# Second feed-forward of a diffusion step: two ordinary hidden pairs in place of three, and its token sums in a new order

## The chip, the cores and the metric

One Trainium2 chip, and one core of it. The metric is the device time of one execution in microseconds (us). The kernel before takes 1400.44 us, the median of 3 runs (1399.87 to 1401.21).

The engines of the core, as the profile names them: PE (TensorE, matmuls), PEld (its weight loads), DVE (VectorE), ACT (ScalarE), POOL (GpSimd) and SP (SyncE, which here issues the loads of weights). Each runs its own list of instructions in the order in which the program writes it, and waits on semaphores for the others.

## What is computed

One trunk layer on 128 context tokens and 512 latent tokens, 1024 channels: a feed-forward, a mixer, and a second feed-forward.

```python
def swiglu(h, w_in, w_out):
    g, u = jnp.split(h @ w_in, 2, axis=-1)
    return (jax.nn.silu(g) * u) @ w_out

def trunk_layer(...):
    h = rms_norm(x, norm_pre[0]) * (1.0 + sc1) + sh1
    x = x + 0.5 * g1 * rms_norm(swiglu(h, ffn_w_in[0], ffn_w_out[0]), norm_post[0])
    h = rms_norm(x, norm_pre[1]) * (1.0 + sc2) + sh2
    m, s_f, s_b = mixer(h, ...)
    x = x + g2 * rms_norm(m, norm_post[1])
    h = rms_norm(x, norm_pre[2]) * (1.0 + sc3) + sh3
    x = x + 0.5 * g3 * rms_norm(swiglu(h, ffn_w_in[1], ffn_w_out[1]), norm_post[2])
```

The hidden width of a feed-forward is 2816, that is 22 blocks of 128 (`FT`); `ffn_w_in` has a gate half and a value half.

## The kernel before, in words

**Numbers in two parts.** Each operand of a matmul is kept as a high part (`_hi`, type fp32r, made by a copy on ACT) and a low part (`_lo`, the full number less the high part, a subtraction on POOL or DVE). A product is three matmuls: high by high, high by low, low by high.

**Tokens** lie in columns, 640 of them (`T`), channels on the partitions in 8 blocks (`KT`). The normalized input of the second feed-forward is in `Hhi` and `Hlo`; it is made in five parts of 128 tokens (semaphores `h_32`, `h_hi`, `h_lo`), of which the last, part 4, is still being made when the feed-forward begins.

**Pairs.** One hidden block needs one slab of gate weights and one of value weights; the two are a pair. The first `EARLY_PAIRS` = 3 pairs are ordinary: in the second feed-forward they run in stage `in1A` over the first 384 tokens (`G_COLS[0]`; pair 0, then the transposes of token part 4, then pairs 1 and 2) and then in stage `in1B` over the other 256 with the weights that were kept. The remaining `SEVEN` = 19 pairs (stage `in1s`, `seven_products`) use seven products of half size in place of eight (Strassen's scheme in Winograd's form): 4 channel blocks by 320 tokens each, 12 matmuls a product, in the order

1. gate rows 0 to 3 by the tokens' quadrant b11,
2. weight sum `s2` by token sum `T2`,
3. `s1` by `T1`,
4. value rows 0 to 3 (by then a weight difference) by `T3`, added to the result of 2,
5. gate rows 4 to 7 by b21, added to 1 (gives `slab_done`),
6. value rows 4 to 7 by `T4` (gives `slab_done`),
7. `s4` by b22, added to 3.

Between them DVE forms the sums U2, U3, C22, C21, C12 out of PSUM and the two halves of the hidden block (`hid_a`, `hid_b`); product 4 waits for U2 and product 7 for C22.

**Token sums** (`token_combinations`, once for each feed-forward `f`): four whole quadrants (`whole`: high plus low) and the sums T1, T2, T3, T4, eight operations of 4 x 320 columns on DVE. ACT makes the high parts of T2, T1 and T4 (`token_highs`) and of T3 (in `seven_gates`), POOL the low parts of T2 and T1 (`token_lows`) and of T4 (in `seven_low`, behind the low half of pair 0's first gate part), DVE that of T3 (in `seven_sums`). The buffer of a token sum's full numbers is that of its low part.

**Weight sums** of a pair: `first_sums` (s1, s2 and the value difference) and `last_sum` (s4) on DVE, `gate_highs` and `value_highs` (seven copies) on ACT, `seven_low` (five subtractions) on POOL, `lows` (s2 and gate rows 4 to 7) on DVE. In the steady state this is done for pair p + 1 while pair p's products run. For pair 0 of the second feed-forward it has to be ready when stage `in1B` ends.

**DVE's order** at the start of the second feed-forward: hidden block (0, 0), then `h_affine(1, 4)` and `h_low(1, 4)` (which complete the input), hidden block (0, 1), the token sums, (0, 2), (1, 0), `first_sums`, `last_sum`, (1, 1), `lows`, (1, 2), and `seven_sums`. (0, 1) is pair 1 of `in1A`, (1, 1) that of `in1B`.

**The end of the pairs.** The hidden blocks lie in `M32`; `whole_high` (ACT) and `whole_low` (DVE) split them for the output product (`out_group`), whose slab m needs blocks 2m and 2m + 1. The ordinary blocks are split while the last pair runs, three more blocks right behind it, and then two for each slab of the output product. Weights go through a few buffers in turn (`STAGES` names them by number); a load waits until the buffer's last user is done (`FREE`), and ACT makes a slab's high part in `after_slab`.

The order on POOL matters below, so these lines of `seven_low` are quoted (564 to 569):

```python
            pool.wait_ge(sem("s_made"), 4 * p + 3)
            pool.wait_ge(sem("seven_hi"), 7 * p + 1)
            low(*(x[:, 0:KH, :] for x in gate)).then_inc(sem("seven_lo"), 1)
            if p == f * SEVEN:
                pool.wait_ge(sem("t_hi"), 3 * f + 3)
                low(*(y[:, :, :] for y in T4)).then_inc(sem("t_lo"), 1)
```

## Time and profile before

| | |
|---|---|
| median of 3 runs | 1400.44 us (1399.87 to 1401.21) |
| span of the profiled execution, first to last instruction | 1397.4 us |
| PE busy | 1376.4 us (98%), 9537 matmuls |
| DVE busy | 747.2 us (53%) |
| POOL busy | 724.6 us (52%) |
| ACT busy | 582.5 us (42%) |
| PE's share of the chain that ended last | 92% |
| second feed-forward, first matmul of each stage | `in1A` 963.88 us, `in1B` 989.76 us, `in1s` 1007.02 us |

The profile's page gives busy times, the chain that ended last and the costliest groups of instructions. The timeline gives single instructions of an engine in order of time, equal neighbours merged; the view of stretches gives each engine's busy time and the granted TensorE clock between two times. All times are us from the start of the span. A matmul's own duration covers its way through the array, so neighbours overlap: what a matmul costs PE is the time from its start to the next one's, and that is read from a stretch divided by the matmuls in it.

### The profile page before, as it was taken

Reading aid. Unit: us, or ns where it says so; the run is one execution under the profiler, and the core shown is the slowest. Engines: PE = TensorE matmul, PEld = TensorE weight load, DVE = VectorE, ACT = ScalarE, POOL = GpSimd, SP = SyncE. Lnnn points to the kernel's source line nnn. Section 1 sums busy time; section 2 is a strip of 40 time slices with the busy share of each in tenths; the row PEclk is TensorE's granted clock in tenths of the full one; section 3 lists DMA queues with packets and bytes.
Section 4 is the critical chain, followed back from the end, with each engine's and each line's share of the span. In section 5 each row is a group of like instructions: output and inputs, shape, how many; then the busy total and the mean of one; then the engine's idle time right before and its main releaser. Section 6 shows DMA issues by size and latency. Waiting matters only on the chain.

```text
span 1397.4 us, 23473 instructions
## 1 busy us (share of the span) xinstructions
PE 1376.4 (98%) x9537; PEld 1257.1 (90%) x9537; DVE 747.2 (53%) x1109; ACT 582.5 (42%) x946; POOL 724.6 (52%) x530
## 2 busy tenths in 40 slices
PE   6999999999999999999999999999999999999998
PEld 5799898999888888999999999988999999998886
DVE  5686565766702431478776312235977666675033
ACT  5243333434534663244445222257344443455243
POOL 0475545465966672324223433542576555667653
PEclk9999999999999999999999999999999999999999
DMA  9756666233545541212112222333122223334465
GB/s 344 263 171 212 218 230 211 61 92 91 177 123 173 189 173 49 61 54 62 54 42 64 76 76 76 103 109 91 46 76 83 77 83 91 91 106 153 135 195 181
DMA packets 215294, 173.34 MB, mean 124 GB/s; under 512 B 6472, under 2 KB 175636, under 8 KB 215060
## 3 DMA queue, kind: packets, MB, share of 16 engines
q1 hardware_dynamic: 212448, 170.61, 39.1%
q8 instruction: 76, 1.25, 0.4%
q10 hardware_dynamic: 2740, 1.24, 0.3%
q14 instruction: 30, 0.25, 0.1%
HBM read 168.65 MB, written 3.17 MB: 123 GB/s over the span
## 4 chain that ended last, share of the span: by engine, by line
PE 92%; DVE 2%; DMA 2%; POOL 2%; ACT 1%; SPq 1%; issue 0%; DVEq 0%; ACTq 0%; POOLq 0%
PE PP L818 33%; PE PP L616 24%; PE PP L635 9%; PE PP L637 9%; PE PP L636 9%; PE PP L674 2%; DMA W_in<-in_ffn_w_in 1%; PE PP L889 1%; PE PP L660 1%; PE PP L1015 1%; PE PP L1031 1%; POOL W_lo L543 0%; DMA W_in<-in_ffn_w_out 0%; PE PP L1085 0%; POOL O_lo L543 0%
## 5 line engine op out<-in xcount | busy, mean ns | idle before, releaser
L543 POOL TENSOR_TENSOR W_lo<-W_in,W_hi 128x512 fp32r<-128x512 f32 (+1 forms) x304 | 380.2, 1277 | 445.2 <-ACT W_hi L1223 437.9
L552 POOL TENSOR_TENSOR W_lo<-W_in,W_hi 128x512 fp32r<-128x512 f32 x112 | 176.2, 1587 | 184.2 <-ACT S_hi L1450 182.3
L1223 ACT ACTIVATE W_hi<-W_in 128x1024 fp32r<-128x1024 f32 x143 | 150.9, 1057 | 224.5 <-PE PP L637 119.9
L635 PE MATMUL PP<-W_hi,Mlo 128*128 128x512 f32 x440 | 172.1, 391 | 0.4 <-DVE W_lo L1850 0.3
L637 PE MATMUL PP<-W_hi,Mhi 128*128 128x512 f32 x440 | 171.3, 389 | 0.0
L636 PE MATMUL PP<-W_lo,Mlo 128*128 128x512 f32 x440 | 171.2, 389 | 0.0
L616 PE MATMUL PP<-Hhi,W_hi 128*128 128x320 f32 (+2 forms) x608 | 146.7, 316 | 0.0
L616 PE MATMUL PP<-Hlo,W_hi 128*128 128x320 f32 (+2 forms) x608 | 142.4, 309 | 0.0
L616 PE MATMUL PP<-Hhi,W_lo 128*128 128x320 f32 (+2 forms) x608 | 142.2, 309 | 0.0
L818 PE MATMUL PP<-Hhi,W_hi 128*128 128x320 f32 x452 | 141.2, 312 | 0.5 <-DVE TT L2007 0.5
L818 PE MATMUL PP<-Hhi,W_lo 128*128 128x320 f32 x452 | 139.7, 309 | 0.0
L818 PE MATMUL PP<-Hlo,W_hi 128*128 128x320 f32 x452 | 139.6, 309 | 0.0
L552 POOL TENSOR_TENSOR S_lo<-S_in,S_hi 128x512 fp32r<-128x512 f32 x76 | 116.1, 1528 | 0.0
L616 PEld LDWEIGHTS PP<-Hhi,W_hi 128*128 128x128 f32 x608 | 101.2, 188 | 3.9 <-issue 2.7
L616 PEld LDWEIGHTS PP<-Hlo,W_hi 128*128 128x128 f32 x608 | 102.8, 188 | 0.0
L616 PEld LDWEIGHTS PP<-Hhi,W_lo 128*128 128x128 f32 x608 | 102.7, 188 | 0.0
L635 PEld LDWEIGHTS PP<-W_hi,Mlo 128*128 128x128 f32 x440 | 82.6, 188 | 19.4 <-POOL W_lo L543 1.0
L637 PEld LDWEIGHTS PP<-W_hi,Mhi 128*128 128x128 f32 x440 | 82.6, 188 | 17.4
L636 PEld LDWEIGHTS PP<-W_lo,Mlo 128*128 128x128 f32 x440 | 82.6, 188 | 16.8
L818 PEld LDWEIGHTS PP<-Hhi,W_hi 128*128 128x128 f32 x452 | 84.8, 188 | 10.8 <-issue 9.9
L818 PE MATMUL PP<-T_hi,S_hi 128*128 128x320 f32 x304 | 93.9, 309 | 0.0
L818 PE MATMUL PP<-T_lo,S_hi 128*128 128x320 f32 x304 | 93.9, 309 | 0.0
(297 smaller groups left out, 3002.1 us busy)
## 6 DMA issues: line engine op xcount, KB each, us to landing
W_in<-in_ffn_w_out SPq DMA_DIRECT2D x176, 256.0 KB, 3.2
W_in<-in_ffn_w_in SPq DMA_DIRECT2D x84, 512.0 KB, 4.3
modl<-in_w_mod SPq DMA_DIRECT2D x14, 2048.0 KB, 8.1
W_in<-in_w_in SPq DMA_DIRECT2D x32, 512.0 KB, 3.8
modw<-in_w_mod SPq DMA_DIRECT2D x4, 2048.0 KB, 14.4
HL<-g_rows SPq DMA_DIRECT2D x6, 512.0 KB, 6.5
V_in<-in_w_in SPq DMA_DIRECT2D x10, 256.0 KB, 3.7
O_in<-in_w_out SPq DMA_DIRECT2D x10, 256.0 KB, 5.6
```

The source lines that it names most:

```text
L543: return nc.gpsimd.tensor_tensor(lo[:, k0:k1, :], full[:, k0:k1, :], hi[:, k0:k1, :].bitcast(fp32), ALU.subtract)
L552: return nc.gpsimd.tensor_tensor(lo, full, hi.bitcast(fp32), ALU.subtract)
L616: m = mm(out[:, 0:c1 - c0], w[:, k, :], src[:, c0:c1], start=lead and n == 0 and a == 0, stop=tail and n == len(x) - 1 and a == 2)
L635: mm(out, xh, wh, start=lead and kk == 0, stop=False)
L636: mm(out, xh, wl, start=False, stop=False)
L637: m = mm(out, xl, wh, start=False, stop=tail and kk == 1)
L660: return nc.tensor.transpose(out, in_, ident[0:k, 0:k])
L674: m = mm(PP[3][32 * q:32 * q + 32, 0, :], S2[:, k, 30 - 2 * i:62 - 2 * i], w[:, k, :], start=first and k < 4, stop=k >= 4, skip_group_chec ...
L818: m = mm(out, wk[:, k, :], xk[:, k, :], start=not add and k == 0 and a == 0, stop=k == KH - 1 and a == 2, skip_group_check=add)
L889: m = mm(PP[n][:, half, 0:HALF], w[:, k, :], src[:, half * HALF:(half + 1) * HALF], start=k == 0 and a == 0, stop=k == KT - 1 and a == 2)
L1015: m = mm(near(pair_of(hd, lev))[32 * q:32 * q + 32, ch, :], KX[lev % 2][:, at:at + 32], queries, start=True, stop=True)
L1223: A(W[i][0], W[i][2], ACT.Copy).then_inc(hi_done, 1)
```

## The change

- `EARLY = (3, 2)`: the second feed-forward has 2 ordinary pairs and 20 pairs with seven products, the first keeps 3 and 19. The counts of semaphores follow from `SEVEN_AT`, `SEVEN_END` and `HIDDEN`.
- Buffers: `in1A` and `in1B` use four; pair 0 of `in1s` uses 12 and 9 as before, pair 1 uses 0 and 8, then 1, 2, 12, 0 in turn.
- DVE, token sums of the second feed-forward: the two quadrants of the first 320 tokens are made ahead of hidden block (0, 0), in the place of T1's and T4's full numbers. After (0, 1) come one quadrant, T1, the other quadrant, T2 and T4. T3 comes later, behind `last_sum`, and hidden block (1, 1) behind `lows`.
- ACT: T1's high part and `gate_highs` after the gate of (0, 1); T2's high part, `value_highs` and then T4's high part after the gate of (1, 0).
- POOL: T1's low part first, then T2's; each waits also until the sums that read the full numbers are made. T4's stays where it was, and T3's stays on DVE.
- At the end of the pairs two blocks are split during the last pair (three before), and the three behind it are 2, 3 and 4 (before: 3, 4 and 5).

```diff
-EARLY_PAIRS = 3
+EARLY = (3, 2)
-SEVEN = FT - EARLY_PAIRS
+SEVEN = tuple(FT - e for e in EARLY)
+SEVEN_AT = (0, SEVEN[0])
+SEVEN_END = (SEVEN[0], SEVEN[0] + SEVEN[1])
+HIDDEN = (EARLY[0], EARLY[0] + EARLY[1], EARLY[0] + 2 * EARLY[1])
...
-    ("in1A", 2 * EARLY_PAIRS, KEEP[:2] + [1, 2, 0] + KEEP[2:3], False),
-    ("in1B", 2 * EARLY_PAIRS, KEEP[:2] + [1, 2, 0] + KEEP[2:3], True),
-    ("in1s", 2 * SEVEN, [12, 9] + [1, 2, 0, 12] * SEVEN, False),
+    ("in1A", 2 * EARLY[1], KEEP[:2] + [1, 2], False),
+    ("in1B", 2 * EARLY[1], KEEP[:2] + [1, 2], True),
+    ("in1s", 2 * SEVEN[1], [12, 9, 0, 8] + [1, 2, 12, 0] * SEVEN[1], False),
...
-            for n, x in enumerate((T2, T1)):
+            for n, x in enumerate(first_tokens(f)):
+                pool.wait_ge(sem("t_made"), 4 * f + (2, 3)[n])
                 pool.wait_ge(sem("t_hi"), 3 * f + n + 1)
                 low(*(y[:, :, :] for y in x)).then_inc(sem("t_lo"), 1)
...
+                if (grp, j) == (0, 1):
+                    token_high(1, T1)
+                    gate_highs(1, 0)
                 if (grp, j) == (1, 0):
-                    token_highs(1)
-                if (grp, j) == (1, 1):
-                    gate_highs(1, 0)
+                    token_high(1, T2)
                     value_highs(1, 0)
+                    token_high(1, T4)
...
+        def second_tokens_first_half():
+            dve.wait_ge(slab_done, BASE["in1A"])
+            dve.wait_ge(sem("h_lo"), NCH + 3)
+            dve.wait_ge(sem("h_hi"), NCH + 3)
+            whole(0, 0, T1[2])
+            link(whole(KH, 0, T4[2]))
+
+        def second_tokens_t1_t2_t4():
+            t3, bsum = T3_IN[1], BSUM[1]
+            dve.wait_ge(sem("h_lo"), 2 * NCH)
+            dve.wait_ge(sem("h_hi"), 2 * NCH)
+            link(whole(0, HALF, t3))
+            V.tensor_tensor(T1[2][:, :, :], t3[:, :, :], T1[2][:, :, :], ALU.subtract).then_inc(sem("t_made"), 1)
+            whole(KH, HALF, bsum).then_inc(sem("b22_whole"), 1)
+            dve.wait_ge(sem("t_made"), 5)
+            dve.wait_ge(sem("b22_whole"), 1)
+            V.tensor_tensor(T2[2][:, :, :], bsum[:, :, :], T1[2][:, :, :], ALU.subtract).then_inc(sem("t_made"), 1)
+            dve.wait_ge(sem("t_made"), 6)
+            V.tensor_tensor(T4[2][:, :, :], T2[2][:, :, :], T4[2][:, :, :], ALU.subtract).then_inc(sem("t_made"), 1)
+
+        def second_tokens_t3():
+            t3, bsum = T3_IN[1], BSUM[1]
+            V.tensor_tensor(t3[:, :, :], bsum[:, :, :], t3[:, :, :], ALU.subtract).then_inc(sem("t_made"), 1)
...
+        second_tokens_first_half()
         early_hidden(0, 0)
         h_affine(1, 4)
         h_low(1, 4)
         early_hidden(0, 1)
-        token_combinations(1)
-        early_hidden(0, 2)
+        second_tokens_t1_t2_t4()
         early_hidden(1, 0)
         first_sums(1, 0)
         last_sum(1, 0)
+        second_tokens_t3()
+        lows(1, 0)
         early_hidden(1, 1)
-        lows(1, 0)
-        early_hidden(1, 2)
         seven_sums(1)
```

## Rows read from the trace of the kernel before

**Rows 1.** The page: busy times, and the chain that ended last, by engine.
```profile
PE 1376.4 (98%) x9537; PEld 1257.1 (90%) x9537; DVE 747.2 (53%) x1109; ACT 582.5 (42%) x946; POOL 724.6 (52%) x530
...
PE 92%; DVE 2%; DMA 2%; POOL 2%; ACT 1%; SPq 1%; issue 0%; DVEq 0%; ACTq 0%; POOLq 0%
```

**Rows 2.** Stretches: start:end, length, PE busy (x matmuls), granted clock, DMA share, GB/s.
```profile
973.02:989.76 16.74, 16.74 (x100) 1.00 0.00 1
989.76:1007.02 17.26, 17.26 (x145) 1.00 0.29 85
1007.02:1020.29 13.27, 12.83 (x86) 1.00 0.17 50
1020.29:1032.61 12.32, 12.32 (x86) 1.00 0.16 45
```

**Rows 3.** Timeline of PE at product 4 of pair 0: start, length, instruction, idle before.
```profile
1012.88 0.41 PE L818 MATMUL PP<-Hhi,I_hi 128*128 128x320 f32 x1 [0.41 <-POOL I_lo L552]
```

**Rows 4.** Timeline of DVE, start of the second feed-forward.
```profile
970.67 0.16 DVE L1829 RECIPROCAL ST<-ST 128x1 f32<-128x1 f32 x1 [1.45 <-ACT ST L1303]
...
978.79 1.22 DVE L1842 TENSOR_TENSOR Hlo<-HL,Hhi 128x1024 fp32r<-128x1024 f32 x1 [1.13 <-ACT Hhi L1313]
981.64 0.56 DVE L2316 TENSOR_TENSOR M<-TT,PP 128x384 f32<-128x384 f32 x1 [1.62 <-PE PP L616]
982.11 1.65 DVE L1908 TENSOR_TENSOR BSUM<-Hhi,Hlo 128x1280 f32<-128x1280 f32 x1
...
985.20 1.49 DVE L1919 TENSOR_TENSOR T_in<-T_in,BSUM 128x1280 f32<-128x1280 f32 x1
...
996.04 0.69 DVE L1937 TENSOR_TENSOR S_in<-I_in 128x512 f32<-128x512 f32 x1
996.76 3.35 DVE L1941 TENSOR_TENSOR S_in<-S_in,W_in 128x512 f32<-128x512 f32 x1
1000.03 3.45 DVE L1942 TENSOR_TENSOR I_in<-W_in,I_in 128x512 f32<-128x512 f32 x1
...
1004.00 0.41 DVE L2316 TENSOR_TENSOR M<-TT,PP 128x256 f32<-128x256 f32 x1
...
1005.71 3.46 DVE L1965 TENSOR_TENSOR W_lo<-W_in,W_hi 128x512 fp32r<-128x512 f32 x1
...
1009.42 2.25 DVE L1996 TENSOR_TENSOR Hlo<-T_in,Hhi 128x1280 fp32r<-128x1280 f32 x1
1011.60 0.47 DVE L2007 TENSOR_TENSOR TT<-TT,PP 128x320 f32<-128x320 f32 x1
```

**Rows 5.** Timeline of POOL, the low parts for pair 0 of `in1s`.
```profile
996.38 6.55 POOL L552 TENSOR_TENSOR T_lo<-T_in,T_hi 128x1280 fp32r<-128x1280 f32 x2 [13.96 <-ACT T_hi L1462]
1003.56 1.69 POOL L552 TENSOR_TENSOR W_lo<-W_in,W_hi 128x512 fp32r<-128x512 f32 x1 [0.63 <-DVE I_in L1942]
1005.19 3.43 POOL L552 TENSOR_TENSOR T_lo<-T_in,T_hi 128x1280 fp32r<-128x1280 f32 x1
1008.59 1.74 POOL L552 TENSOR_TENSOR S_lo<-S_in,S_hi 128x512 fp32r<-128x512 f32 x1
1010.29 4.24 POOL L552 TENSOR_TENSOR I_lo<-I_in,I_hi 128x512 fp32r<-128x512 f32 x2
```

**Rows 6.** Timeline of ACT, high parts: of the token sums, of pair 0.
```profile
995.04 3.58 ACT L1462 ACTIVATE T_hi<-T_in 128x1280 fp32r<-128x1280 f32 x3
...
998.87 1.14 ACT L1442 ACTIVATE W_hi<-W_in 128x512 fp32r<-128x512 f32 x2
```

**Rows 7.** Timelines of PE and DVE: first feed-forward's output product, slabs 0 to 2.
```profile
343.93 0.39 PE L635 MATMUL PP<-W_hi,Mlo 128*128 128x512 f32 x1
...
351.13 3.54 DVE L1983 TENSOR_TENSOR Mhi<-M,Mlo 128x640 fp32r<-128x640 f32 x2 [3.00 <-ACT Mlo L1355]
...
352.29 0.47 PE L635 MATMUL PP<-W_hi,Mlo 128*128 128x512 f32 x1
```

**Rows 8.** Stretches of PE alone behind its last matmul, columns as in rows 2.
```profile
1391.90:1396.30 4.40, 0.01 (x1) 1.00 0.56 218
1396.30:1397.40 1.10, 0.00 (x0) 0.51 0.21 80
```

More of the change, by code:

```diff
@@ L123, in plan @@
         free[base["woA"] + n] = after
-    for n, after in ((0, base["woA"]), (1, base["woA"] + 1)) + ((5, base["in1A"] - 1),):
+    for n, after in ((0, base["woA"]), (1, base["woA"] + 1)):
         free[base["in1A"] + n] = after
@@ L128, in plan @@
     free[base["in1s"] + 1] = base["in1A"] - 1
+    free[base["in1s"] + 3] = base["in1A"] - 1
     return base, buf, free, order, need, fresh
@@ L368, in early_bank, with first_tokens @@
         return ((4, 0), (6, 2))[grp][j % 2] + u
+    def first_tokens(f):
+        return (T1, T2) if f else (T2, T1)
     def ring_entries():
@@ L373, in ring_entries @@
         entries = []
-        for _ in range(SEVEN):
+        for _ in range(max(SEVEN)):
             entries.append((RING[s1], RING[s2], RING[s4]))
@@ L485, in _ @@
         load(BASE["in0s"], 0, KT, w0[:, :, j * P:(j + 1) * P])
-        for p in range(1, SEVEN):
-            j = EARLY_PAIRS + p
+        for p in range(1, SEVEN[0]):
+            j = EARLY[0] + p
             load_pair(BASE["in0s"] + 2 * p, w0, j)
@@ L520, in _ @@
         w1 = ffn_w_in[0, 1].rearrange("(k p) n -> p k n", p=P)
-        for j in range(EARLY_PAIRS):
+        for j in range(EARLY[1]):
             load_pair(BASE["in1A"] + 2 * j, w1, j)
-        for j in range(EARLY_PAIRS, FT):
-            load_pair(BASE["in1s"] + 2 * (j - EARLY_PAIRS), w1, j)
+        for j in range(EARLY[1], FT):
+            load_pair(BASE["in1s"] + 2 * (j - EARLY[1]), w1, j)
         wo1 = ffn_w_out[0, 1].rearrange("(k p) n -> p k n", p=P)
@@ L584, in _ @@
             if i in (BASE["out0A"], BASE["out1A"]):
-                for p in range(SEVEN):
+                for p in range(SEVEN[int(i == BASE["out1A"])]):
                     seven_low(int(i == BASE["out1A"]), p)
@@ L843, in seven_products @@
                 pe.wait_ge(sem("hid_a"), p - 1)
+            if first and f:
+                pe.wait_ge(sem("gate_ready"), HIDDEN[1])
             product(x, quadrant(gate, 0, KH), b11).then_inc(sem("product"), 1)
@@ L918, in _ @@
         late_mods(2)
-        for j in range(1, EARLY_PAIRS):
+        for j in range(1, EARLY[0]):
             if j == 1:
@@ L934, in _ @@
         last_mod = MOD_LATE - len(MOD_AFTER) - 1
-        for p in range(SEVEN):
+        for p in range(SEVEN[0]):
             seven_products(0, p)
@@ L1181, in _ @@
         pe.wait_ge(sem("h_lo"), NCH + 3)
-        for j in range(EARLY_PAIRS):
+        for j in range(EARLY[1]):
             if j == 0:
@@ L1197, in _ @@
         pe.wait_ge(sem("h_lo"), 2 * NCH)
-        for j in range(EARLY_PAIRS):
+        for j in range(EARLY[1]):
             for u in range(2):
@@ L1202, in _ @@
                 if j > 1:
-                    pe.wait_ge(sem("hid_ready" if u else "gate_ready"), 2 * EARLY_PAIRS + j - 1)
+                    pe.wait_ge(sem("hid_ready" if u else "gate_ready"), HIDDEN[1] + j - 1)
                 slab(i, (bank(early_bank(1, j, u)),), h_tiles, (G_COLS[1],)).then_inc(slab_done, 1)
-        for p in range(SEVEN):
+        for p in range(SEVEN[1]):
             seven_products(1, p)
@@ L1334, in out_group @@
                 if b != 1 and grp == 0:
-                    for j in range(EARLY_PAIRS + 2 * m + 3, min(FT, EARLY_PAIRS + 2 * m + 5)):
+                    e = EARLY[b // 2]
+                    for j in range(e + 2 * m + 3, min(FT, e + 2 * m + 5)):
                         whole_high(b // 2, j)
@@ L1470, in seven_gates @@
             act.wait_ge(slab_done, BASE[SEVENTHS[f]])
+            act.wait_ge(sem("t_made"), 4 * f + 4)
             A(T3[0], T3_IN[f][:, :, :], ACT.Copy).then_inc(sem("t3_hi"), 1)
-            for p in range(SEVEN):
+            for p in range(SEVEN[f]):
                 i, _, _ = seven_slabs(f, p)
                 x = seven_banks(f, p)[0]
-                n = f * SEVEN + p
+                n = SEVEN_AT[f] + p
                 if p:
@@ L1486, in seven_gates @@
                 else:
-                    for j in range(EARLY_PAIRS):
+                    for j in range(EARLY[f]):
                         whole_high(f, j)
@@ L1504, in _ @@
             if j == 1:
-                token_highs(0)
+                for x in (T2, T1, T4):
+                    token_high(0, x)
             if j == 2:
@@ L1693, in _ @@
             c0, c1 = G_COLS[grp]
-            for j in range(EARLY_PAIRS):
-                n = (1 + grp) * EARLY_PAIRS + j
+            for j in range(EARLY[1]):
+                n = HIDDEN[grp] + j
                 after_slab(BASE[stage] + 2 * j)
@@ L1910, in token_combinations @@
         def token_combinations(f):
[L1911 to L1915 removed]
+            dve.wait_ge(sem("h0_ready"), KT)
             t3, bsum = T3_IN[f], BSUM[f]
@@ L1996, in seven_sums @@
             V.tensor_tensor(T3[1], T3_IN[f][:, :, :], T3[0].bitcast(fp32), ALU.subtract).then_inc(sem("t3_lo"), 1)
-            for p in range(SEVEN):
+            for p in range(SEVEN[f]):
                 i, _, _ = seven_slabs(f, p)
                 x, y, z, v = seven_banks(f, p)
-                n = f * SEVEN + p
+                n = SEVEN_AT[f] + p
                 if p:
@@ L2022, in seven_sums @@
                 V.tensor_tensor(A_C22, A_U3, z, ALU.add).then_inc(sem("c22_done"), 1)
-                if p + 1 < SEVEN:
+                if p + 1 < SEVEN[f]:
                     lows(f, p + 1)
                 else:
-                    whole_low(f, 1)
-                    whole_low(f, 2)
+                    for j in range(1, EARLY[f]):
+                        whole_low(f, j)
                 dve.wait_ge(slab_done, i + 2)
```

94 lines of the change are left out of this document (43 added, 51 removed).

## The prediction

> **What bounds the kernel now.** I read the page first. PE is busy for 98% of the span and holds 92% of the chain that ended last [rows 1], so the time is the number of PE's matmuls by their pitch, plus the few stalls of PE. An edit can win only by taking matmuls off PE, and lose only by making PE wait. Next I read PE's pitch in both kinds of pair from the view of stretches, which shows the 384-column, 256-column and 320-column stages apart [rows 2]. Last I read the timelines of DVE, POOL and ACT from 970 to 1012 us, where pair 0 of the seven-product stage is prepared, and asked how much earlier than PE each piece is ready. That slack is small: product 4 of pair 0 already starts late behind POOL's low half of the value slab [rows 3]. It starts at 1012.88 where 36 matmuls behind 1007.02, at 0.147 us each, would put it at 1012.30; there is no slack left at this point.
>
> **What the change takes off PE.** An ordinary pair is 48 matmuls of 384 columns and 48 of 256. 973.02 to 989.76 holds two pairs of the first kind, 8.37 us each; 989.76 to 1007.02 holds three of the second, 5.75 us each [rows 2]. Together 14.12 us. A seven-product pair is 84 matmuls in 12.32 us, the last stretch of that view [rows 2]. One pair changes its kind, so PE saves 14.12 - 12.32 = 1.80 us, with everything else hidden. That is all there is to win, 0.13%. But stage in1s now begins 14.12 us earlier, at 1007.02 - 14.12 = 992.90, and the preparation of pair 0 has to be done 14.12 us earlier too.
>
> **When the preparation can begin.** The input is complete with the last low part at 978.79 + 1.22 = 980.0 [rows 4]. The early half of the token sums, two operations of about 1.5 us, fits behind 970.83, where DVE is idle until hidden block (0, 0); I cost it at nothing, and if that idle time were gone it would cost nothing still, since DVE next waits for PE at 981.64 [rows 4]. This wait does not move: it is for pair 1 of in1A. From the start of the next operation at 982.11 [rows 4] I walk the new order, at a pitch of 1.5 us per token operation:
> - DVE: quadrant to 983.7, T1 to 985.2, quadrant to 986.7, T2 to 988.2, T4 to 989.7, hidden block (1, 0) to 990.1 (0.41 us [rows 4]).
> - ACT: T1's high part (3.58 us for three, so 1.2 us [rows 6]) to 986.5, then gate_highs, T2's high part to 989.5.
> - POOL may write T1's low part only when T2 is made, 988.2. Before, the first token low part started at 996.38 [rows 5]. The two-part order thus gains 8.1 us here, not 14.12.
>
> **How DVE and POOL share.** A low part of 1280 columns takes POOL 3.28 us (6.55 for two [rows 5]). DVE's weight sums of 512 columns take 0.69 us when POOL is idle and 3.35 and 3.45 us when POOL makes token low parts [rows 4]: each ends about half a microsecond behind the end of a POOL operation (996.38 + 3.28 = 999.66, against 1000.11; 1002.93 against 1003.48). So I count one such DVE operation per POOL operation. Hidden blocks and PSUM sums stay at 0.41 to 0.5 us beside a busy POOL (1004.00 in [rows 4] lies inside 1003.56 to 1005.25 in [rows 5]). The Trainium skill, SBUF — State Buffer, section "Who interferes with whom", says that a DVE instruction with two SBUF inputs and a GpSimd one that reads SBUF exclude each other, the second to issue waiting for the first. By it, too, moving DVE's sums beside POOL's token low parts buys little.
>
> **Pair 0, step by step.**
> 1. T4 and T1's low part become ready together at 988.2; whichever goes first, T1's low part and T2's are done at about 996.2 (988.2 + 1.5 + 3.2 + 3.4).
> 2. DVE: s1 gets through at 993.4, s2 at 996.8, the value difference, with POOL idle, at 997.5.
> 3. POOL: gate rows 0 to 3 wait for that difference: 997.6 + 1.69 [rows 5] = 999.25. **PE's product 1 starts at 999.3 where it could at 992.90: a stall of 6.4 us.** Before, this low part was ready at 1005.25, 1.8 us ahead of PE.
> 4. ACT: value_highs is five copies from 996.9 at a pitch of 0.52 us (two take 1.14, one 0.62 [rows 6]), and T4's high part stands behind them, to 1000.8. POOL, in order, waits for it, then takes 3.43 us [rows 5]: T4's low part done at 1004.3. Before: 1008.62.
> 5. From here the pattern of before repeats, 4.2 to 4.3 us earlier: s1's low part (1.74), value rows (2.1 each) [rows 5]; DVE's gate rows 4 to 7 (3.46), T3's low part (2.25), U2 (0.47) [rows 4]. T3 and s2's low part fit between 998 and 1001.3, so product 2 runs behind product 1.
> 6. Product 3 waits for s1's low part, 1006.1. Product 4 starts at 1012.88 - 4.2 = **1008.7**; without any stall it would be 992.90 + 5.28 = 998.2. PE has lost 10.5 us there.
>
> Behind product 4 both kernels do the same with the same neighbours: 12.32 us for the added pair, and what was at 1012.88 is at 1008.7. Shift so far: -4.2 + 12.32 = +8.1 us.
>
> **The end of the pairs.** With two ordinary blocks, block 5 leaves the group of three behind the last pair and becomes the first of slab 0's two, and output slab 2 waits for it. The buffers of the new order also free the third output slab half a pair later. The first feed-forward has that buffer order now: its first block of that place is split from 351.13, two in 3.54 us, and slab 2 starts at 352.29 [rows 7], 0.17 us late by the pitch of 0.227 us (36 matmuls behind 343.93, the stage's first [rows 7]), held by the weights. There it was block 6, which slab 2 doesn't need; block 5 would be ready at 351.13 + 1.7 = 352.85. I take 0.7 us; bounds 0 (the split uncontended, 0.8 us) and 1.5 us (it waits for one POOL operation more). SP's loads move with the slabs' users; pair 1's two are free when the mixer's output ends, before 970 us, so no load is on the path. I cost that at nothing; a late load would be 2 us at most (within the upper end).
>
> **The sum.** 8.1 + 0.7 = +8.8 us. The profiled execution has a span of 1397.4 us and the median of the runs is 1400.44, 3.0 us more; I add the shift to both: span 1406.2, **1409.2 us** for the median.
>
> **Bounds of the preparation.** The long DVE operations are the unknown. Below: none of them waits (rival 2), +2.5 us. Above: POOL loses another 1.5 us to DVE in T1's and T2's low parts and one DVE operation (3.4 us) lands ahead of U2: +12.
>
> **The rivals.**
> 1. *Hidden after all* (the other side: not slower). If pair 0's gate low part is ready by 992.90 and the others keep PE's pace, the change gives -1.80 + 0.7 = -1.1: 1399.3 us. It decides at that one time. For it speaks only that DVE and POOL are about half idle over the span [rows 1]. Against it: T2 is made at 988.2, and the two token low parts (6.5 us) and a gate part (1.3 us) stand in POOL's queue before it, 996.0 even without contention. Chance 4%.
> 2. *POOL's queue without the exclusion*: T1 and T2 low to 994.7, gate to 996.0, T4 to 999.2, s1 to 1000.5, value rows 0 to 3 to 1001.8, products 3 and 4 from 1000.6 and 1002.4. Then 1002.4 - 1012.88 + 12.32 + 0.7 = +2.5: 1402.9 us. The durations of 3.35 to 3.46 us speak against it. Chance 8%.
> 3. *The clock falls in the stall.* Behind PE's last matmul, near 1391.9, the granted clock is 1.00 up to 1396.30 and 0.51 behind [rows 8], so behind 4.4 us of idleness PE fell to 1.2 GHz there, and the stall is 6.4. At half the clock products 1 and 2 would take 3.5 us each: product 3 would start at 1006.3 against 1006.1, and if it is slow too, product 4 at 1009.8. Cost 0 to 1.5 us, so 1410.5 us. Most of it hides in the wait that is there anyway. The Trainium skill, TensorE: Matmul & The Clock Gate, section "HAM oscillation — how this bites in real kernels", describes this chain of wait and slow restart; it speaks against the change. Chance 20%.
> 4. *The preparation takes longer than the copied pattern*: 1411 to 1413 us, chance 8%.
>
> **How the numbers follow.** My forecast has 60%. Its own range is 1406.5 to 1411.5. The range is 1403.5 to 1412.5, which leaves out rivals 1 and 2 and part of 4. Within 0.2% (2.8 us, about what a measurement of this kernel can tell from no change) is 1397.6 to 1403.2: rivals 1 and 2, 11%. Faster by more isn't reached even with all hidden; I keep 1% of rival 1's 4 for it, for an output stage that gains as well. Slower: 88%.
>
> **What the new profile would show.** PE idle from about 992.9 to 999.3 ahead of the first 320-column matmul of in1s, released by POOL's low part of the gate slab; a second gap ahead of product 3 (some 3 us) and a small one ahead of product 4; T1's low part starting near 988.3; DVE's s1 and s2 near 3.3 us long; a gap of POOL near 999 to 1001 ended by T4's high part; pair 1's first matmul near 1016; a short gap at output slab 2. I am wrong if s1 and s2 take 0.7 us beside the token low parts, or if product 1 starts before 997.

## The result, and the profile after

The changed kernel takes 1408.24 us, the median of 4 runs (1407.34 to 1409.29), against 1400.64 us for the kernel before beside it (4 runs, 1399.87 to 1401.21). The ratio is 1.0059, with a 95% interval of 1.0047 to 1.0071: 7.6 us slower, 0.54%, where 8.8 us were forecast. The profiled execution has a span of 1406.5 us at a mean granted clock of 0.996. It is slower, and by nearly the forecast amount; but two of the terms were off in opposite directions, and one rival, the fall of the clock, came true in its first part.

The page of the changed kernel first, its busy times and its chain, to be read against [rows 1]:

```profile
PE 1377.5 (98%) x9525; PEld 1257.7 (89%) x9525; DVE 753.4 (54%) x1120; ACT 584.6 (42%) x952; POOL 729.3 (52%) x531
...
PE 90%; DVE 3%; DMA 2%; ACT 2%; POOL 1%; SPq 1%; issue 1%; DVEq 0%; ACTq 0%; POOLq 0%
```

PE has 12 matmuls fewer (one pair's 96 have become 84) and its share of the chain falls from 92% to 90%. Its busy time has not fallen, although it does less, since part of it ran at half the clock. The groups of PE's waits say where it stood still. Columns: engine and tile, line, who ended the wait, total us, times, longest.

```profile
PE PP L827 <- POOL W_lo L560: 5.6, 1, 5.6
PE PP L644 <- DVE Mhi L2021: 2.4, 3, 1.6
...
PE PP L827 <- POOL I_lo L560: 0.5, 1, 0.5
```

The first line is product 1 of pair 0 waiting for the low half of the gate slab. The second is mostly in the output product, which had no wait for DVE in its first slabs before. The third is product 4. PE's timeline places them (start, length, instruction, idle before):

```profile
991.97 0.28 PE L625 MATMUL PP<-Hhi,W_lo 128*128 128x256 f32 x1
997.84 0.63 PE L827 MATMUL PP<-Hhi,W_hi 128*128 128x320 f32 x1 [5.58 <-POOL W_lo L560]
...
1003.94 0.31 PE L827 MATMUL PP<-T_hi,S_lo 128*128 128x320 f32 x1
1004.26 0.41 PE L827 MATMUL PP<-T_hi,S_hi 128*128 128x320 f32 x1
...
1006.76 0.41 PE L827 MATMUL PP<-Hhi,I_hi 128*128 128x320 f32 x1 [0.48 <-POOL I_lo L560]
...
1256.22 0.39 PE L646 MATMUL PP<-W_hi,Mhi 128*128 128x512 f32 x1
1257.22 0.50 PE L644 MATMUL PP<-W_hi,Mlo 128*128 128x512 f32 x1 [0.61 <-DVE Mhi L2021]
...
1277.53 0.39 PE L646 MATMUL PP<-W_hi,Mhi 128*128 128x512 f32 x1
1279.53 0.50 PE L644 MATMUL PP<-W_hi,Mlo 128*128 128x512 f32 x1 [1.62 <-DVE Mhi L2021]
```

The last matmul of `in1B` starts at 991.97; at its pitch of 0.12 us product 1 could start at 992.09 and starts at 997.84: 5.7 us lost. Product 3 follows product 2 at 1004.26, product 4 starts at 1006.76 where it started at 1012.88 before [rows 3]. Output slab 2 loses 0.77 us (1257.22 - 1256.22 - the pitch of 0.227), slab 7 loses 1.77 (1279.53 - 1277.53 - 0.227).

What made product 1 late is in the timelines of DVE and POOL, which answer to [rows 4] and [rows 5]:

```profile
985.77 1.49 DVE L1957 TENSOR_TENSOR T_in<-BSUM,T_in 128x1280 f32<-128x1280 f32 x1
987.30 1.49 DVE L1959 TENSOR_TENSOR T_in<-T_in 128x1280 f32<-128x1280 f32 x1
988.71 0.41 DVE L2352 TENSOR_TENSOR M<-TT,PP 128x256 f32<-128x256 f32 x1
989.04 3.12 DVE L1975 TENSOR_TENSOR S_in<-I_in 128x512 f32<-128x512 f32 x1
992.20 3.25 DVE L1979 TENSOR_TENSOR S_in<-S_in,W_in 128x512 f32<-128x512 f32 x1
995.37 0.68 DVE L1980 TENSOR_TENSOR I_in<-W_in,I_in 128x512 f32<-128x512 f32 x1
```

```profile
987.34 7.56 POOL L560 TENSOR_TENSOR T_lo<-T_in,T_hi 128x1280 fp32r<-128x1280 f32 x2 [12.10 <-DVE T_in L1957]
996.13 1.65 POOL L560 TENSOR_TENSOR W_lo<-W_in,W_hi 128x512 fp32r<-128x512 f32 x1 [1.23 <-DVE I_in L1980]
999.44 3.07 POOL L560 TENSOR_TENSOR T_lo<-T_in,T_hi 128x1280 fp32r<-128x1280 f32 x1 [1.66 <-ACT T_hi L1473]
```

POOL starts T1's low part when DVE has made T2 (985.77 + 1.49 = 987.26), does both token parts in 7.56 us, and is free at 994.90. DVE's s1 and s2 take 3.12 and 3.25 us beside it, the value difference 0.68 behind it. The gate's low part waits for that difference, runs from 996.13 to 997.78, and product 1 starts 0.06 us later.

**Which time to hold the sum against.** In the profile of after the first matmul of `in1A` comes at 963.04, before at 963.88. Nothing ahead of it was edited, and over the thirteen profiled executions of this study it lies between 962.97 and 964.83. So below I give times from that matmul (t = 0), read from each kernel's timeline of PE:

| kernel | product 1 | product 4 | output product | end of span | output to end |
|---|---|---|---|---|---|
| before | 43.14 | 49.00 | 278.17 | 433.53 | 155.36 |
| after | 34.80 | 43.72 | 285.22 | 443.47 | 158.25 |

Product 4 comes 5.28 us sooner and one seven-product pair of 12.32 us [rows 2] is added behind it: +7.04, and the output product starts at +7.05. From there to the end the changed kernel loses 2.89 us more. Together +9.94 us in the part that was edited. The metric shows 7.6. Of the difference, 0.84 us is the upstream scatter between the two profiled executions, which leaves +9.1 between their spans (1406.5 - 1397.4). Some 0.4 us lies outside the span: 1.76 to 1.84 us in all four executions of after, 2.19 to 2.30 us in 43 executions of the kernel before that ran beside the experiments. The rest would be that the profiled execution of before was a short one: with 2.2 us outside, the median execution of before has a span near 1398.4, 1.0 us above the profiled one's 1397.4. But the spans of those four executions are not on record, and the 1.0 is worked out from their median, so 9.94 - 0.84 - 1.0 - 0.4 = 7.7 closes by construction and shows nothing.

The later runs speak for the larger number. The two kernels of the section on the clock take the same time from t = 0 to the end as the changed kernel within 0.2 us (443.27 and 443.63 against 443.47), and they are 9.0 and 9.7 us slower than the kernel before on their own chips. The interval of the changed kernel reaches from 6.6 to 9.9 us and holds both. So the loss is 7.6 us as measured here, and probably nearer the 9.5 (9.94 - 0.4) of the traces.

### The profile page after: what moved, and what is told of

Same layout as the page of the kernel before. It is cut to its first block, busy times and chain, and to the rows that moved or that the text cites. A ratio compares the mean times of both kernels' runs of the same rounds, so it can differ in the third digit from the quotient of the medians.

```text
span 1406.5 us, 23487 instructions
## 1 busy us (share of the span) xinstructions
PE 1377.5 (98%) x9525; PEld 1257.7 (89%) x9525; DVE 753.4 (54%) x1120; ACT 584.6 (42%) x952; POOL 729.3 (52%) x531
## 4 chain that ended last, share of the span: by engine, by line
PE 90%; DVE 3%; DMA 2%; ACT 2%; POOL 1%; SPq 1%; issue 1%; DVEq 0%; ACTq 0%; POOLq 0%
PE PP L827 34%; PE PP L625 23%; PE PP L644 8%; PE PP L646 8%; PE PP L645 8%; PE PP L683 2%; PE PP L900 1%; DMA W_in<-in_ffn_w_in 1%; PE PP L669 1%; PE PP L1026 1%; DMA W_in<-in_ffn_w_out 1%; PE PP L1042 1%; POOL W_lo L551 0%; DVE Mhi L2021 0%; PE PP L1096 0%
## 5 line engine op out<-in xcount | busy, mean ns | idle before, releaser
L827 PE MATMUL PP<-Hhi,W_hi 128*128 128x320 f32 x460 | 144.4, 314 | 6.0 <-POOL W_lo L560 5.6
L827 PE MATMUL PP<-Hhi,W_lo 128*128 128x320 f32 x460 | 142.8, 310 | 0.0
L827 PE MATMUL PP<-Hlo,W_hi 128*128 128x320 f32 x460 | 142.7, 310 | 0.0
L625 PE MATMUL PP<-Hhi,W_hi 128*128 128x320 f32 (+2 forms) x592 | 141.7, 316 | 0.0
L625 PE MATMUL PP<-Hlo,W_hi 128*128 128x320 f32 (+2 forms) x592 | 137.4, 309 | 0.0
L625 PE MATMUL PP<-Hhi,W_lo 128*128 128x320 f32 (+2 forms) x592 | 137.3, 309 | 0.0
L560 POOL TENSOR_TENSOR S_lo<-S_in,S_hi 128x512 fp32r<-128x512 f32 x78 | 119.3, 1530 | 0.0
L625 PEld LDWEIGHTS PP<-Hlo,W_hi 128*128 128x128 f32 x592 | 99.6, 188 | 0.0
L827 PE MATMUL PP<-T_hi,S_hi 128*128 128x320 f32 x312 | 97.0, 311 | 0.0
L827 PE MATMUL PP<-T_hi,S_lo 128*128 128x320 f32 x312 | 96.9, 311 | 0.0
```

Of the source, the lines that this page charges most:

```text
L560: return nc.gpsimd.tensor_tensor(lo, full, hi.bitcast(fp32), ALU.subtract)
L625: m = mm(out[:, 0:c1 - c0], w[:, k, :], src[:, c0:c1], start=lead and n == 0 and a == 0, stop=tail and n == len(x) - 1 and a == 2)
L827: m = mm(out, wk[:, k, :], xk[:, k, :], start=not add and k == 0 and a == 0, stop=k == KH - 1 and a == 2, skip_group_check=add)
```

## The experiments

The question was not whether it is slower but which of the edits costs, and whether the mechanism named in the prediction is the one: DVE and POOL excluding each other in front of pair 0 (my theory), or POOL's queue alone, or the clock. All diffs are against the changed kernel. The three groups of runs were on different chips; ratios are to runs of the kernel before on the same chip (medians 1400.15, 1398.88 and 1399.93 us). Times in us of different groups can't be set side by side, only what each kernel is over its own before.

Most effects below are 2 to 3 us, and four executions of a kernel scatter by up to 4 us, so they are read from t = 0 in one profiled execution of each kernel. The medians do not show them: the changed kernel is 7.6 us over before, and the four kernels whose traces are 2.0 to 3.1 us shorter from t = 0 are 7.5 (one more split), 8.3 (without T4's low part), 6.8 (sums first) and 8.4 us (low parts on DVE) over theirs.

### The two halves of the change

The new order with the old number of pairs (the buffers of the stages and the loads' order go back too):

```diff
-EARLY = (3, 2)
+EARLY = (3, 3)
...
         second_tokens_t1_t2_t4()
+        early_hidden(0, 2)
         early_hidden(1, 0)
...
         early_hidden(1, 1)
+        early_hidden(1, 2)
```

> Three ordinary pairs as before, with the new order of token sums and high and low parts. Theory (POOL's queue of low parts bounds pair 0, and the new order starts it earlier): token low parts start near 988 in place of 996.4, all of pair 0's low parts are ready before PE's product 1, the stall of 0.57 us ahead of product 4 and that of 0.2 us ahead of product 7 go, nothing else moves: 0.5 to 0.8 us faster than before, about 1399.9 us. Rival (the order itself costs, for instance by the early sums delaying the last token part): 1401 us or more.

Measured: 1398.29 us (10 runs), ratio 0.9987, interval 0.9978 to 0.9997. The order alone is not slower; it is a trifle faster. In its trace product 4 comes at t = 48.41 against 49.00 before, the output product at 277.21, 0.96 us sooner. The two small waits of pair 0 are gone, since T1's low part starts at t = 24.5, eight us sooner than the first token low part before (996.38 [rows 5], t = 32.5), while PE arrives no sooner (t = 43.13):

```profile
987.49 4.27 POOL L559 TENSOR_TENSOR T_lo<-T_in,T_hi 128x1280 fp32r<-128x1280 f32 x1 [5.95 <-DVE T_in L1956]
...
998.49 1.68 POOL L559 TENSOR_TENSOR W_lo<-W_in,W_hi 128x512 fp32r<-128x512 f32 x1 [1.95 <-DVE I_in L1979]
```

The gate's low part is ready at 1000.17, some 6 us ahead of PE.

The two pairs with the old order of the sums (the orders of high parts on ACT and of low parts on POOL go back too):

```diff
-        second_tokens_first_half()
         early_hidden(0, 0)
...
-        second_tokens_t1_t2_t4()
+        token_combinations(1)
         early_hidden(1, 0)
         first_sums(1, 0)
         last_sum(1, 0)
-        second_tokens_t3()
-        lows(1, 0)
         early_hidden(1, 1)
+        lows(1, 0)
```

> Two ordinary pairs, with the order of token sums, high and low parts of before. Theory: eight token operations end near 993.3, token low parts on POOL start near 994.6, and product 4 of pair 0 starts 3 to 4 us later than in the changed kernel: about 1412 us, 11 to 12 us over before; so the new order wins back some 3.5 of the 14 us by which the preparation would have to be earlier. Rival (the order makes no difference once POOL is full): 1408 us as the changed kernel.

Measured: 1412.24 us (4 runs), ratio 1.0084, interval 1.0067 to 1.0100. PE's waits in its second feed-forward:

```profile
PE PP L826 <- POOL W_lo L560: 10.4, 1, 10.4
PE PP L643 <- DVE Mhi L2023: 2.3, 2, 1.6
```

Product 1 waits 10.4 us in place of 5.6, product 4 starts at t = 47.13, 3.41 us behind the changed kernel's 43.72. From t = 0 to the end it takes 446.86 us, 13.3 more than before, where the changed kernel takes 9.9 more. So the change of one pair costs more than the whole loss, and the new order pays back a quarter of it, 3.4 us. The waits in the output product are there again, with the old order: they come with the pair as well.

### What holds product 1

One quadrant and T1 ahead of hidden block (0, 1), so that DVE begins the token sums without waiting for PE:

```diff
             V.tensor_tensor(T1[2][:, :, :], t3[:, :, :], T1[2][:, :, :], ALU.subtract).then_inc(sem("t_made"), 1)
+            early_hidden(0, 1)
             whole(KH, HALF, bsum).then_inc(sem("b22_whole"), 1)
...
-        early_hidden(0, 1)
         second_tokens_t1_t2_t4()
```

> The changed kernel, with one quadrant and T1 made ahead of hidden block (0, 1) on DVE, which waits for PE: they can start 2.8 us earlier, as soon as the input is complete. Theory (the chain from the first token sum over POOL to product 4 is unbroken, so an earlier start is passed on in full): product 1 and product 4 of pair 0 both 2.5 us earlier, 1405.7 us. Rival (POOL's or ACT's later waits absorb it): product 4 moves less than 1 us.

Measured: 1405.72 us (4 runs), ratio 1.0049, interval 1.0034 to 1.0064. Product 1 at t = 32.36 and product 4 at 41.28, both 2.44 us sooner than in the changed kernel:

```profile
985.18 7.62 POOL L560 TENSOR_TENSOR T_lo<-T_in,T_hi 128x1280 fp32r<-128x1280 f32 x2 [9.62 <-DVE T_in L1958]
994.03 1.65 POOL L560 TENSOR_TENSOR W_lo<-W_in,W_hi 128x512 fp32r<-128x512 f32 x1 [1.23 <-DVE I_in L1981]
```

T2 is made 2.50 us sooner, and all of pair 0 that follows moves with it. PE's stall is what lies between T2 and its arrival. At the end of the span 2.06 us are left of the 2.44, because slab 7 of the output product waits 2.05 us here in place of 1.62. That the median agrees with the expected 1405.7 is chance: this chip's kernel before takes 1398.88 us, so the run is 6.8 us over it and only 0.8 us better than the changed kernel's 7.6.

T1's and T2's low parts on DVE, which leaves POOL idle while DVE makes the weight sums:

```diff
-            for n, x in enumerate(first_tokens(f)):
+            for n, x in enumerate(first_tokens(f) if f == 0 else ()):
...
         second_tokens_t1_t2_t4()
+        for n, x in enumerate((T1, T2)):
+            dve.wait_ge(sem("t_made"), 7)
+            dve.wait_ge(sem("t_hi"), 4 + n)
+            V.tensor_tensor(x[1][:, :, :], x[2][:, :, :], x[0][:, :, :].bitcast(fp32), ALU.subtract)\
+                .then_inc(sem("t_lo"), 1)
         early_hidden(1, 0)
```

> The changed kernel, with the low parts of T1 and T2 on DVE (1.5 us each) and not on POOL (3.2 us each). Theory (one engine of the two works at a time, so what counts is their summed time, and POOL is the slow one): DVE's weight sums s1 and s2 take 0.7 us in place of 3.1 and 3.25, product 1 starts about 2.2 us earlier, product 4 about 2 us earlier (it then waits for T4's high part, which stands behind five copies on ACT), 1406.2 us. Rival (DVE is the bound, and work put on it delays everything): the same or slower than the changed kernel, 1408 to 1411 us.

Measured: 1407.25 us (4 runs), ratio 1.0061, interval 1.0044 to 1.0078. Product 1 at t = 32.75, product 4 at 41.67, both 2.05 us sooner. DVE's timeline in it:

```profile
989.48 2.89 DVE L2364 TENSOR_TENSOR T_lo<-T_in,T_hi 128x1280 fp32r<-128x1280 f32 x2
...
992.62 0.68 DVE L1975 TENSOR_TENSOR S_in<-I_in 128x512 f32<-128x512 f32 x1
993.34 0.69 DVE L1979 TENSOR_TENSOR S_in<-S_in,W_in 128x512 f32<-128x512 f32 x1
```

This is the cleanest sight of the exclusion: s1 and s2, the same instructions, take 0.68 and 0.69 us with POOL idle and 3.12 and 3.25 with POOL making the token low parts. The two low parts cost DVE 2.89 us where POOL needs 7.56. The rule of the Trainium skill, SBUF — State Buffer, section "Who interferes with whom", that a DVE instruction with two SBUF inputs and a GpSimd one that reads SBUF take turns, the later waiting for the whole of the other, agrees with these rows; so does its other half, that one with at most one SBUF input does not contend: the hidden block, of which one input is in PSUM, takes 0.41 us in either kernel. The median moved less than the trace: the ratio is no lower than that of the changed kernel, and the intervals of the two (0.24% and 0.34% wide) can't separate 2 us.

### What holds products 3 and 4

T4's low part left out (POOL subtracts only 32 columns, and product 6 of the second feed-forward uses T4's high part in the low one's place, so T4's low half is missing from what is computed):

```diff
-                low(*(y[:, :, :] for y in T4)).then_inc(sem("t_lo"), 1)
+                low(*((y[:, :, :] if f == 0 else y[:, 0:1, 0:32]) for y in T4)).then_inc(sem("t_lo"), 1)
...
-            product(v, quadrant(value, KH, KT), T4).then_inc(slab_done, 1)
+            product(v, quadrant(value, KH, KT), (T4[0], T4[0]) if f else T4).then_inc(slab_done, 1)
```

> The changed kernel without T4's low part in the second feed-forward: POOL makes a 1 x 32 corner of it in place of 4 x 320 columns, and product 6 takes the high part twice, with the same number of matmuls, so the output is not the exact product. Theory (POOL's queue of low parts, in its order, bounds products 3 and 4 of pair 0): POOL saves 3.1 us, and DVE's low half of gate rows 4 to 7 no longer waits behind it; product 4 starts 2.5 to 3.0 us earlier, 1405.4 us. Rival (DVE's chain of T3 low and U2 bounds product 4 anyway): less than 1 us.

Measured: 1407.19 us (4 runs, 1405.56 to 1409.75), ratio 1.0060, interval 1.0045 to 1.0075. Product 1 stays at t = 34.78, product 4 comes at 41.51, 2.21 us sooner:

```profile
999.79 0.42 POOL L560 TENSOR_TENSOR T_lo<-T_in,T_hi 128x32 fp32r<-128x32 f32 x1 [1.65 <-ACT T_hi L1473]
```

POOL still waits 1.65 us for T4's high part, because the instruction is still in its queue. The step of the prediction holds: T4's low part stands on the path to product 4. Its 2.65 us (3.07 - 0.42) came back as 2.21. The rest is PE's own: the low part of the value slab was ready at 1004.42 and product 4 started at 1004.93 without a wait, behind a product 1 that had run at half the clock. So here, where POOL is out of the way, the slow clock does cost, some 0.5 us. Its four runs spread by 4.2 us, too much for the median to show it.

### The output product

ACT splits one more hidden block ahead of the output product (four behind the last pair in place of three, and each later one a place sooner):

```diff
-            for j in range(EARLY[f], EARLY[f] + 3):
+            for j in range(EARLY[f], EARLY[f] + 3 + f):
                 whole_high(f, j)
...
-                    e = EARLY[b // 2]
+                    e = EARLY[b // 2] + b // 2
```

> The changed kernel, with one more hidden block split ahead of the output product of the second feed-forward (four behind the last pair in place of three, and the groups of two that follow start one block later). Theory (both stalls of the output product, 0.77 us at slab 2 and 1.78 us at slab 7, come from the lead of one block that two ordinary pairs took away): slab 2 waits 0.2 us, slab 7 not at all, 2.0 to 2.5 us faster than the changed kernel, about 1405.9. Rival (slab 7 waits for its weights, whose load comes late): only 0.6 us, 1407.6.

Measured: 1407.63 us (4 runs), ratio 1.0052, interval 1.0037 to 1.0067. From the output product to the end it takes 156.22 us in place of 158.25: 2.0 us less. Slab 7's wait is gone, and PE has one left there:

```profile
PE PP L644 <- POOL W_lo L551: 0.6, 1, 0.6
```

That is slab 2, as long as before the edit but with another releaser. The fourth split stands on ACT ahead of the high part of slab 2's weights. ACT in after, and then in this kernel:

```profile
1249.42 1.98 ACT L1367 ACTIVATE Mlo<-M 128x640 fp32r<-128x640 f32 x3
...
1252.82 1.99 ACT L1234 ACTIVATE W_hi<-W_in 128x1024 fp32r<-128x1024 f32 x2
...
1270.76 1.35 ACT L1367 ACTIVATE Mlo<-M 128x640 fp32r<-128x640 f32 x2
1276.38 1.06 ACT L1234 ACTIVATE W_hi<-W_in 128x1024 fp32r<-128x1024 f32 x1 [4.28 <-DMA W_in<-in_ffn_w_out]
1277.35 1.35 ACT L1367 ACTIVATE Mlo<-M 128x640 fp32r<-128x640 f32 x2
```

```profile
1250.84 2.61 ACT L1367 ACTIVATE Mlo<-M 128x640 fp32r<-128x640 f32 x4
...
1254.87 1.99 ACT L1234 ACTIVATE W_hi<-W_in 128x1024 fp32r<-128x1024 f32 x2
```

Four copies take 2.61 us in place of 1.98. Block 5, for which slab 2 had waited, is now ready some 4 us sooner, but slab 2's weights become ready 0.6 us later and hold PE just as long. So the theory was right for slab 7 and wrong for slab 2. That the median of 1407.63 is the rival's 1407.6 says nothing: it is 7.5 us over its chip's before, no better than the changed kernel, and the trace has the 2.0 us.

The rows of after also show what slab 7 waited for: ACT stood 4.28 us for a slab of weights, with the split of block 15 queued behind it, at 1277.35. Before, ACT waited for loads there too:

```profile
1264.49 1.06 ACT L1223 ACTIVATE W_hi<-W_in 128x1024 fp32r<-128x1024 f32 x1 [3.58 <-DMA W_in<-in_ffn_w_out]
1265.46 1.35 ACT L1355 ACTIVATE Mlo<-M 128x640 fp32r<-128x640 f32 x2
1269.35 1.06 ACT L1223 ACTIVATE W_hi<-W_in 128x1024 fp32r<-128x1024 f32 x1 [2.54 <-DMA W_in<-in_ffn_w_out]
```

With three ordinary pairs block 15 is split one slab earlier, at 1265.46, which is 23.4 us behind the output product's first matmul; after it is 29.1 us behind. Slab 7 begins some 28.6 us behind, so before even the longer wait of 3.58 us was covered. The two loads of gains, which SP issues between slabs (1259.62 before, 1266.73 after), may be what makes the slab's load late; no run tested that.

### The clock

In the changed kernel the clock was granted at half from 996.87 to 1003.69. The stretches of after's PE (columns as in [rows 2]):

```profile
992.00:996.00 4.00, 0.25 (x3) 1.00 0.57 167
996.00:1000.00 4.00, 2.16 (x8) 0.61 0.00 0
1000.00:1004.00 4.00, 4.00 (x18) 0.54 0.00 0
1004.00:1008.00 4.00, 3.51 (x22) 1.00 0.00 0
```

So rival 3 came true in its first part: product 1 and most of product 2 ran at 1.2 GHz. Whether it costs anything needs a run in which the clock stays up. PE is given 44 more matmuls of 256 columns, whose result nobody reads, ahead of product 1:

```diff
+            if first and f:
+                pe.wait_ge(sem("hid_ready"), HIDDEN[1])
+                for _ in range(44):
+                    mm(bank(5)[:, 0:256], Hhi[:, 0, 0:P], Hhi[:, 0, 0:256], start=True, stop=True)
```

> The changed kernel, with 44 extra matmuls of 256 columns (result not used) on PE while it waits for product 1 of pair 0, so that the clock stays at 2.4 GHz. Theory (product 4 is bound by POOL's low part of the value slab, and what the clock costs hides in that wait): products 1 and 2 are faster, product 4 starts at the same time, 0.0 us, within 0.3. Rival (the fall of the clock costs what products 1 to 3 lose at 1.2 GHz): 1.0 to 1.7 us faster than the changed kernel.

Measured: 1409.19 us (4 runs), ratio 1.0064, interval 1.0049 to 1.0079. The clock fell all the same, only later:

```profile
1001.00:1006.00 5.00, 2.71 (x18) 1.00 0.00 0
1006.52:1009.93 3.41, 3.41 (x15) 0.50 0.00 0
```

Products 1 and 2 ran at full speed, product 3 then waited 2.45 us for POOL's low part of s1, and half the clock fell on product 3, which has no wait to hide in: product 4 at t = 44.41, 0.7 us later than in the changed kernel. This was inconclusive on the price, so a second version fills that wait too:

```diff
+            if first and f:
+                for _ in range(20):
+                    mm(bank(1)[:, 0:256], Hhi[:, 0, 0:P], Hhi[:, 0, 0:256], start=True, stop=True)
```

> The kernel of e4_clock_kept, with 20 more extra matmuls of 256 columns between products 2 and 3 of pair 0, so that no gap of more than 1 us is left for PE there. Theory: the granted clock stays at 1.00 from in1A on, product 4 starts 43.7 us behind in1A's first matmul as in the changed kernel (44.4 in e4, where the clock fell during product 3), so the fall of the clock costs the changed kernel nothing. Rival (it costs something): product 4 at 43.2 us or earlier.

Measured: 1409.63 us (4 runs), ratio 1.0070, interval 1.0056 to 1.0084, at full clock throughout:

```profile
996.00:1000.00 4.00, 3.60 (x29) 1.00 0.21 64
1000.00:1004.00 4.00, 4.00 (x30) 1.00 0.02 4
1004.00:1008.00 4.00, 3.73 (x27) 1.00 0.00 0
```

Product 1 at t = 34.90, product 4 at 43.87, against 34.80 and 43.72 with the fall. The end is at 443.63 against 443.47. In the changed kernel the slow clock cost nothing: POOL decides when products 3 and 4 start, and the slow products only used up a wait. Where nothing else holds those products it does cost: 0.7 us in the run with only the first wait filled, some 0.5 us without T4's low part.

### Everything that helped, together

Sums first, T1's and T2's low parts on DVE, the fourth split, and T4's high part ahead of `value_highs`:

```diff
                     token_high(1, T2)
-                    value_highs(1, 0)
                     token_high(1, T4)
+                    value_highs(1, 0)
```

> The changed kernel with four edits at once: sums ahead of hidden block (0, 1), T1's and T2's low parts on DVE, T4's high part ahead of value_highs on ACT, and one more hidden block split ahead of the output product. Theory (stalls of pair 0 add to those of the output product): product 1 starts 1 to 2 us after PE is ready, product 4 some 5 us earlier than in the changed kernel, slab 7 doesn't wait: 7 to 8 us faster than the changed kernel, about 1401, which is no gain over before. Rival (contention of DVE with T4's low part gives most of it back): 1403 to 1404.

Measured: 1403.25 us (6 runs), ratio 1.0029, interval 1.0018 to 1.0041. It wins back half, and is still slower than the kernel before. Product 1 is at t = 30.24 with 1.0 us of waiting left, but product 4 is at 40.05, 3.67 us sooner where 5 were expected. PE now waits at product 2:

```profile
PE PP L827 <- DVE S_lo L2001: 2.6, 1, 2.6
PE PP L827 <- POOL W_lo L560: 1.0, 1, 1.0
```

DVE's low part of s2, which product 2 needs, and POOL's low part of T4 meet. DVE's timeline, then POOL's:

```profile
995.25 3.39 DVE L2001 TENSOR_TENSOR S_lo<-S_in,S_hi 128x512 fp32r<-128x512 f32 x1
```

```profile
993.93 4.15 POOL L560 TENSOR_TENSOR T_lo<-T_in,T_hi 128x1280 fp32r<-128x1280 f32 x1
```

The same operation of DVE takes 0.68 us in the changed kernel, where POOL was waiting for T4's high part at that moment. Moving T4's high part forward closed a gap of POOL that DVE had been using (with the sums first or the low parts on DVE alone the gap is there, and the operation takes 0.68 us). The clock has a share too: from 998.70 to 1002.00 it was granted at 0.53, PE has no wait between product 2 and product 4 at 1003.84, and U2 was ready at 1003.20. So up to 0.6 us of the missing 1.3 is the slow clock's.

### Is the order alone faster?

The order with three pairs once more, in five rounds, and with the sums first:

> Three ordinary pairs with the new order of token sums, high and low parts (the kernel of e1_order_only), in more rounds. In the profile of e1_order_only the stretch from stage in1A's first matmul to the end was 0.95 us shorter than in before, of which the two stalls of pair 0 (0.57 and 0.2 us) are 0.77. Theory (that is all the order gives, the rest of e1's 1.9 us is scatter upstream of in1A): 0.7 to 1.1 us faster than before, ratio near 0.9993. Rival (the order changes something upstream as well): 1.9 us again, ratio 0.9987 with an interval that leaves 0.9993 out.

> The kernel of e1_order_only, with one quadrant and T1 ahead of hidden block (0, 1) as in e6_sums_first. Theory (with three ordinary pairs the preparation is ahead of PE everywhere, so an earlier start is worth nothing): same as e9_order_again within 0.3 us. Rival: another 1 us or more faster.

Measured: 1398.71 us (11 runs), ratio 0.9991, interval 0.9982 to 1.0000, and 1398.49 us (11 runs), ratio 0.9990, interval 0.9981 to 0.9999. In both, product 4 is at t = 48.42 and 48.44 and the output product at 277.22 and 277.24: 0.93 to 0.95 us sooner than before, with no wait of PE left in pair 0, so bringing the sums forward again has nothing to win. The medians differ by 1.2 and 1.4 us, of which 0.4 lies outside the span (1.76 to 1.87 us outside, against 2.20 to 2.30 for the kernel before), and the rest is the 0.9 us of the trace. These two are the only forms found here that aren't slower than the kernel before, and they keep the three pairs; their gain of 0.1% is at the edge of what these runs can tell.

## Why the prediction was right, point by point

**PE's saving of 1.80 us** holds: 12 matmuls fewer, PE could start product 1 at t = 29.05 (992.09 - 963.04), 14.09 us sooner than before, and the added pair is 12.32 us long, as the step from -5.28 to +7.05 shows.

**When the preparation can begin.** T1's low part was put 24.3 us behind the first matmul of `in1A` (988.2 - 963.88), and started at 24.30. The first half of the sums was costed at nothing and was hidden in DVE's idle time. The reason given, that POOL waits for T2, is confirmed by sums first, where moving T2 moved everything.

**How DVE and POOL share.** Forecast: one long DVE operation for each of POOL's. Measured: 3.12 and 3.25 us beside the token parts, 0.68 when POOL is idle, in one kernel and again across two. The 0.69 us that I read before as one with POOL idle was not quite that: the operation ran from 996.04 to 996.73 and POOL began at 996.38, so it was the first of the two. Rival 2, without the exclusion, is refuted by the same rows.

**Pair 0** was mis-sized by 1.1 us, too pessimistic. Product 1 was forecast at t = 35.4 and came at 34.80, after 5.7 us of stall and not 6.4: the token low parts took 7.56 us and not the 8.0 I allowed (8.1 by the terms I added), because I put a whole DVE operation of 1.5 us ahead of the first, and the first took 4.27 us, 1.2 more than the 3.07 of T4's. T4's low part was given the 3.43 us that its row of before has and took 3.07. Product 4 was forecast 4.2 us sooner than before and came 5.28 sooner.

**Rival 3, the clock,** was given 20% and a cost of 0 to 1.5 us. The clock fell, from 996.87 to 1003.69, and its cost in this kernel is nought within 0.2 us (the run with filled waits). My remark that most of it hides in the wait for s1's low part was right, and it also removes the "gap of some 3 us ahead of product 3" that I said the profile would show: 0.17 us is left of it (1004.26 - 1003.94 - 0.147), the rest being products run slowly.

**Behind product 4** both kernels do the same: +12.32 was to give +8.1 at the output product and gave +7.05, all of the difference being product 4's.

**The end of the pairs** is the step that failed. I took 0.7 us, bounds 0 to 1.5, for slab 2. Slab 2 lost 0.77, released by DVE's split of a hidden block, as forecast. But the stage lost 2.89, nearly twice my upper bound, since slab 7 lost 1.77 at a place that I never looked at; 0.1 us more went at the matmul behind each wait. I followed the lead of the splits only to the end of the group behind the pairs; it is one block shorter at every slab from there on, and a place where ACT waits long for a load uses it up. In the runs with two pairs and three splits slab 7 waits between 0.47 and 2.05 us, and in the run with both waits filled slab 10 waits 0.93 as well: where the lead runs out moves with the loads. The traced rows that would have shown it were there before the change: ACT waiting 3.58 and 2.54 us for slabs' loads, with splits queued behind. I had priced a late load at 2 us at most, but within the upper end and only for the pairs.

**The sum** of +8.8 thus stands against +9.94 in the edited part of the profiled executions: +1.1 us too much in pair 0, 2.2 too little in the output product. That the median moved by 7.6 owes more to 0.4 us outside the span and to scatter that these few executions can't resolve. The sign of the loss and its place are explained; that the forecast came so near is partly luck, since the two errors partly cancel in the sum and the scatter did the rest. **Rival 1** (hidden after all) was wrong at the point named: the gate's low part was ready at 997.78, PE there at 992.09.

What stays open: why the program of before has 0.4 us more outside its span, why the executions of one kernel scatter by a microsecond or two ahead of `in1A`, and what makes the load ahead of slab 7 late.

## What to carry to other kernels

Work that is taken off the bounding engine ahead of a stage also takes away the time in which that stage is prepared. Subtract it from each piece's slack first: here 1.8 us of matmuls saved moved PE's arrival 14 us forward against a slack of 1.8, and reordering the preparation returned 3.4 of the 13.3 us that this cost. When a lead (of splits, of loads) becomes one step shorter, go through every later place where the leading engine waits, not only the first consumer. And an engine pair that takes turns has to be scheduled as one queue: closing a gap of POOL lengthened the DVE operation that had used it from 0.68 to 3.39 us.

## What the runs showed of the hardware

- The clock. In the changed kernel the last matmul ahead of the wait started at 991.97 and the next at 997.84; the clock fell at 996.87, inside the wait, and was at half until 1003.69. With sums first it stayed at full through waits of 3.12 us and, a few microseconds later, 2.45 us. With the first wait filled by matmuls, it fell 0.36 us after the end of a single wait of 2.45 us. So the length of the longest wait alone did not decide here.
- POOL's 1280-column subtraction took 2.95 to 3.43 us in most places and 4.15 to 4.27 us where a DVE operation of 1.5 us or more on SBUF was under way at its start; DVE's took 1.45 us (2.89 for two).
- What lies outside the span is a property of the program, steady within 0.1 us over 43 executions, and differs between programs by 0.4 us: in a comparison of 0.1% it is a third of the difference.
